# Where the second layer's memory keys and values are computed: in the first layer, or between expert quads

## The chip, the cores and the metric

The kernel runs on one core of a Trainium2 chip. The metric is the device time of one execution in microseconds. Three runs of the kernel before took 991.36, 989.58 and 991.78 us; the median is 991.36 us.

## The reference, cut to what matters

Two transformer layers follow each other on 256 tokens of width 1024. The first has a mixer, a cross attention to a memory of 256 rows and a mixture of 32 experts. The second is a hybrid layer; one of its three branches is a cross attention to another memory, `mem_2`.

```python
def reference(...):
    x = first_block(x, mem, ...)      # mixer, cross attention, experts
    return second_block(x, mem_2, ...)
# in first_block, per layer
    h = h + _mixer(...)
    h = h + _cross_attention(h, mem, ...)          # softmax over 256 rows, 4 heads, then @ w_out
    h = h + _hier_moe(h, ...)                      # router, then hid = silu(xb @ w_gate[e]) * (xb @ w_up[e]); hid @ w_down[e]
# in hybrid_layer
    kv = rmsnorm(mem, g_mem) @ w_mem_kv            # 256 x 1024 by 1024 x 1024
    xk = kv[..., :X_W].reshape(B, M, X_HEADS, X_HEAD_DIM)      # keys: the first 512 columns
    xv = kv[..., X_W:].reshape(B, M, X_HEADS, X_HEAD_DIM)      # values: the last 512
    yc = cross_attention(heads(xq, ...), xk, xv)
```

`xk` and `xv` depend on the inputs alone, so they can be computed at any time before the second layer's cross attention.

## The kernel before

**Dense blocks.** Every dense weight matrix is used in blocks of 1024 x 512 (2 MiB in fp32, two halves of 1 MiB). SP loads the halves, in the order of `FIRST_BLOCKS` and `SECOND_BLOCKS`, into a raw ring (`load_dense`, L694 is its DMA), each when the block two places earlier has been used. ACT rounds a half to a high part (`split_hi`, L1021), VectorE makes the low part (`split_lo`, L1600), and TensorE forms three products: high by high, high by low, low by high (`dense`, L2697 to L2699, or `moving_by_quarters`, L2723 to L2726). A block is 48 matmuls with 512 moving columns, or 96 with 256 where the weights stand (`standing`). The last blocks of the first layer are cq0, cq1 (queries), xk2 (the second layer's memory keys), co0, co1 (output of the cross attention) and xv2 (the second layer's memory values).

**Order on TensorE at the end of the first layer.** The queries are turned and the scores cs formed (L3026). ACT and VectorE make the softmax of four heads in two pairs (maxima L1806, exponentials L1044, weights L2058). Meanwhile TensorE runs xk2, with the transposes of the first two heads' probabilities between its halves (`turn_first_probs`). Four fp32 outputs follow (`co_0` to `co_3`, L3057), then co0 and co1. Then comes xv2, in four quarters. The transposes of the new h, the router's logits (L3079) and the ranks (L3090 to L3094) are put between its steps (`router_before`, `logits_behind`), so that VectorE's router work (L2114 to L2189) goes on beside it. The row norm factors of the memory are spread over partitions by two small matmuls (mrow0, mrow1, L2658).

**Experts.** The 32 experts are worked in eight quads of four. Each expert has room for 32 tokens. A quad's weights are six units of 4 MiB: gate, gate, up, up, down, down (24 MiB a quad). TensorE gathers the tokens (L3127), uses the units (fp32 matmuls, L3155 for gate and up, L3178 for down, 32 records a unit), and scatters the outputs (L3212). There are four unit buffers, so SP (`load_quad`, L735) may issue unit g when unit g - 4 has been used; it learns that from the semaphore `unit_used`. Buffer 1 is used by units 1 of the first quad and 0 of the second; the first two experts' pieces of the second quad's first unit have a place of their own, `ahead`. The first quad's pieces are loaded in parts during the first layer, each as soon as its place is free: `load_piece` (L728), `load_staged` (down weights in places of their own, L760 and L763), `load_part` (L794), the last gate piece (L811) and the last down pieces (L816, L839). L839 is issued when TensorE has used half of the first unit (`first_used`). The remaining piece of the second quad's first unit is issued when the sixth unit is used (L846). SP's queue is worked strictly in order: a wait holds everything behind it.

**After the experts** the second layer's dense blocks follow; xk2 and xv2 are first read near its end.

## Time and profile before

| | value |
|---|---|
| median of three runs | 991.36 us |
| the profiled execution | 989.82 us, span of its instructions 988.0 us |
| TensorE busy | 834.9 us (85%) |
| VectorE, ScalarE, GpSimd busy | 481.3, 335.2, 23.4 us |
| DMA | 294.71 MB, mean 298 GB/s |
| granted TensorE clock, mean | 0.938 |
| chain that ended last | PE 59%, DMA 35%, ACT 2%, DVE 2% |

PE is TensorE, DVE VectorE, ACT ScalarE, POOL GpSimd, SP the queue that issues most DMAs. All times in the rows are microseconds from the start of the span of the profiled execution, which is the one to make sums against. Its time outside the span is 1.8 us. Matmuls are pipelined: the busy time of one (0.39 us for 512 columns) is longer than the distance from one to the next (0.23 us), so stages are measured from start to start. A share of the DMA engines is the part of the time in which the 16 engines had packets, averaged over them.

### The profile page before, as it was taken

To read this page: it belongs to the slowest core of one execution; us is meant where nothing else is said; L and a number is where in the kernel's file an instruction comes from. 1 tells how busy PE (TensorE), PEld (TensorE's weight loads), DVE (VectorE), ACT (ScalarE), POOL (GpSimd) and SP (SyncE) were. 2 spreads that over 40 slices of the span, in tenths; PEclk is the share of its full clock that TensorE was granted. 3 is DMA by queue.
4 is the path that set the end of the run, shared out by engine and by line. 5 is a ranking of instruction groups with operands and counts; after the bars stand their busy time and mean duration, and the time that the engine had idled before them with its cause. 6 is when DMAs were issued, how large, how long until landed. Compare 5 with 4: busy or idle time off the path is not lost.

```text
span 988.0 us, 12917 instructions
## 1 busy us (share of the span) xinstructions
PE 834.9 (85%) x5185; PEld 576.2 (58%) x5185; DVE 481.3 (49%) x946; ACT 335.2 (34%) x560; POOL 23.4 (2%) x35
## 2 busy tenths in 40 slices
PE   8999999999986665757566585747999999999997
PEld 8788888898631211313121131312887899888996
DVE  5788767774611120302003030201867788787695
ACT  5666745854110000101010010001434656455533
POOL 1021010100000000000000000000000000000000
PEclk9999999999997888978888887879999999999999
DMA  8754666597999999999999999999555445453531
GB/s 311 277 171 170 212 223 229 186 410 277 375 429 424 433 429 429 433 429 432 432 428 433 427 431 430 425 436 393 194 170 172 143 155 160 139 170 130 194 130 60
DMA packets 64155, 294.71 MB, mean 298 GB/s; under 512 B 3970, under 2 KB 16996, under 8 KB 55396
## 3 DMA queue, kind: packets, MB, share of 16 engines
q1 hardware_dynamic: 62644, 290.91, 74.9%
q10 hardware_dynamic: 1456, 3.03, 0.8%
q8 instruction: 39, 0.64, 0.3%
q14 instruction: 16, 0.13, 0.0%
HBM read 292.88 MB, written 1.05 MB: 297 GB/s over the span
## 4 chain that ended last, share of the span: by engine, by line
PE 59%; DMA 35%; ACT 2%; DVE 2%; SPq 2%; issue 1%; POOL 0%; POOLq 0%; ACTq 0%; DVEq 0%
DMA uT<-in_down_units 11%; PE bank L2697 10%; PE bank L2699 10%; PE bank L2698 10%; DMA uT<-in_gate_units 10%; DMA uT<-in_up_units 10%; PE bank L3155 5%; PE bank L2762 5%; PE bank L2631 3%; PE bank L3178 3%; PE bank L2764 2%; DMA ring<-in_first_blocks 2%; DMA ring<-in_gate_units 2%; PE bank L3269 1%; PE bank L3476 1%; PE bank L2912 1%
## 5 line engine op out<-in xcount | busy, mean ns | idle before, releaser
L1600 DVE TENSOR_TENSOR ring_rounded<-ring,ring_rounded 128x2048 fp32r<-128x2048 f32 x76 | 174.2, 2292 | 87.1 <-ACT ring_rounded L1021 86.5
L1021 ACT ACTIVATE ring_rounded<-ring 128x2048 fp32r<-128x2048 f32 x75 | 143.6, 1914 | 154.2 <-PE bank L2699 118.9
L3155 PE MATMUL bank<-ring,main 128*32 128x512 f32 x744 | 106.7, 704 | 47.7 <-DMA ring<-in_up_units 43.2
L2699 PE MATMUL bank<-ring_rounded 128*128 128x512 f32 x320 | 124.9, 390 | 0.0
L3155 PEld LDWEIGHTS bank<-ring,main 128*32 128x32 f32 x744 | 27.5, 126 | 115.2 <-issue 92.3
L2697 PE MATMUL bank<-ring_rounded,uT_rounded 128*128 128x512 f32 x208 | 82.8, 398 | 0.7 <-DVE ring_rounded L1600 0.5
L2698 PE MATMUL bank<-ring_rounded,uT_rounded 128*128 128x512 f32 x208 | 81.1, 390 | 0.0
L3178 PE MATMUL bank<-ring,main 128*32 128x512 f32 x352 | 50.5, 726 | 34.4 <-DMA ring<-in_down_units 34.4
L2762 PE MATMUL bank<-stream_pair,ring_rounded 128*128 128x512 f32 x192 | 69.6, 405 | 0.0
L2223 DVE TENSOR_TENSOR normed<-bank,normed 128x512 f32<-128x512 f32 x20 | 13.8, 692 | 110.5 <-PE bank L3212 110.5
L2699 PEld LDWEIGHTS bank<-ring_rounded 128*128 128x128 f32 x320 | 60.1, 188 | 12.9
L2200 DVE SCALAR_TENSOR_TENSOR main<-main,bank 128x512 f32<-128x512 f32 x8 | 5.5, 688 | 125.2 <-PE bank L3155 125.2
L3155 PE MATMUL bank<-main 128*32 128x512 f32 x200 | 40.0, 718 | 22.3 <-DMA uT<-in_up_units 13.5
L2764 PE MATMUL bank<-stream_pair,ring_rounded 128*128 128x256 f32 x192 | 53.8, 280 | 0.0
L1320 ACT ACTIVATE main<-bank 128x512 f32<-128x512 f32 x8 | 4.8, 597 | 143.3 <-PE bank L2631 143.3
L3178 PEld LDWEIGHTS bank<-ring,main 128*32 128x32 f32 x352 | 13.3, 129 | 66.4 <-issue 38.4
L2697 PE MATMUL bank<-ring_rounded 128*128 128x512 f32 x128 | 51.0, 399 | 0.0
L1328 ACT ACTIVATE main<-bank 128x512 f32<-128x512 f32 x16 | 9.6, 598 | 121.6 <-PE bank L3178 121.6
L2698 PE MATMUL bank<-ring_rounded 128*128 128x512 f32 x128 | 49.9, 390 | 0.0
L2697 PEld LDWEIGHTS bank<-ring_rounded,uT_rounded 128*128 128x128 f32 x208 | 39.0, 188 | 11.7 <-DVE ring_rounded L1600 2.1
L2698 PEld LDWEIGHTS bank<-ring_rounded,uT_rounded 128*128 128x128 f32 x208 | 39.1, 188 | 7.4
L2762 PEld LDWEIGHTS bank<-stream_pair,ring_rounded 128*128 128x128 f32 x192 | 36.1, 188 | 10.7 <-issue 2.4
(381 smaller groups left out, 1582.0 us busy)
## 6 DMA issues: line engine op xcount, KB each, us to landing
ring<-in_up_units SPq DMA_DIRECT2D x11, 4096.0 KB, 33.5
ring<-in_w_in SPq DMA_DIRECT2D x42, 1024.0 KB, 5.1
ring<-in_down_units SPq DMA_DIRECT2D x10, 4096.0 KB, 32.2
ring<-in_gate_units SPq DMA_DIRECT2D x9, 4096.0 KB, 33.5
main<-in_gate_units SPq DMA_DIRECT2D x4, 3072.0 KB, 30.3
main<-in_down_units SPq DMA_DIRECT2D x3, 3072.0 KB, 32.6
main<-in_up_units SPq DMA_DIRECT2D x3, 3072.0 KB, 30.4
ring<-in_w_ckv SPq DMA_DIRECT2D x8, 1024.0 KB, 5.1
```

Of the source, the lines that this page charges most:

```text
L1021: a.activation(rounded(hi_half(name, h)), raw_half(name, h), ACT.Copy).then_inc(hi_made, 1)
L1600: v.tensor_tensor(rounded(raw), raw, as_f32(hi_half(name, h)), ALU.subtract).then_inc(split_made, 1)
L2223: ins = v.tensor_tensor(to, b[:, :], to, ALU.add)
L2631: return nc.tensor.transpose(dst, src, ident[0:k, 0:k])
L2697: mm(dst, left[0], right[0], start=first, stop=False, skip_group_check=True)
L2698: mm(dst, left[0], right[1], start=False, stop=False, skip_group_check=True)
L2699: last = mm(dst, left[1], right[0], start=False, stop=last_one, skip_group_check=True)
L2762: mm(b[:, :, :], w_hi[:, k, at], low_and_high(k), start=k == 0, stop=False, skip_group_check=True)
L2764: last = mm(b[:, 1, :], w_lo[:, k, at], x_hi[:, k, :], start=False, stop=k == KC - 1, skip_group_check=True)
L2912: ins = mm(banks[n][:, t * P:t * P + (t + 1) * P], left[on, t * P:(t + 1) * P], right[on, 0:(t + 1) * P], start=t == 0, stop=True, skip_gr ...
L3155: last = mm(bank[2 + part][on, :], xg3[:, h * (KC // 2) + k, on], expert_piece(j, p, u, e, KC)[:, k, :], start=h + k == 0, stop=h * (KC // ...
L3178: ins = mm(bank[4 + half][on, :], hidT3[:, c, on], w[:, half * 512:half * 512 + 512], start=c == 0, stop=c == FC - 1)
```

## The change

The blocks xk2 and xv2 leave the first layer and the plan of dense blocks; `co0` and `co1` each move up in the loads. TensorE computes keys and values as plain fp32 products instead of three products of rounded parts: the keys between quad 0 and quad 1 (`memory_keys`: 32 matmuls of 256 moving columns, after the scatter of quad 0), the values between quad 1 and quad 2 (`memory_values`: 16 of 512 columns). Their weights are loaded by SP in the experts' stream: the keys' 2 MiB into the part of buffer 1 that the second quad leaves free, behind L843; the values' 2 MiB into `ahead`, behind the wait until the second quad's first unit has been used. The last two units of the second quad stand behind that and behind a wait for the finished keys. ACT multiplies the transposed memory by its gain after quad 0, and moves row factors and values; VectorE spreads the factors after quad 0 and moves the keys. So each has its second quad written out ahead of its loop.

The softmax of the cross attention has no dense block beside it any more: the heads are turned and multiplied in pairs. In the router, transposes, logits and ranks follow each other, with 14 and 6 dummy matmuls (`keep_busy`) before the two waits for VectorE. Two copies of h2T go from ACT to VectorE. The rounding of the memory into high and low parts (`raw_hi`, `raw_lo`) goes; the transposed memory lands where the raw copy had its high part.

The places that this frees let SP issue earlier: the first quad's last gate piece (1 MiB) behind cq0, one staged half (0.5 MiB), an up piece (1 MiB) and a whole staged piece (1 MiB) behind co0, and the other gate pieces of unit 1 beside co0 and co1. The banks of PSUM are renumbered by a constant shift (`expert_bank`). The diff, cut to its core:

```diff
-FIRST_PARTS = (4, 8, 4, 8)
+FIRST_PARTS = (4, 5, 4, 8)
...
-                "wo0", "wo1", "cq0", "cq1", "xk2", "co0", "co1", "xv2"]
+                "wo0", "wo1", "cq0", "cq1", "co0", "co1"]
...
+        key_weights = ring[:, 0:SLOT].rearrange("p (k n) -> p k n", k=KC)
+        value_weights = ahead[:, :].rearrange("p (k n) -> p k n", k=KC)
...
+                    sp.dma_start(expert_piece(0, 0, 1, GROUP - 1, KC), of_expert(gate_w, GROUP - 1, 1, KC))\
+                        .then_inc(unit_landed[1], 16)
                 elif name == "co0":
-                    wait_filled(sp, LAST_USE["cq1"])
-                    load_piece(0, 1, gate_w)
+                    load_staged(2, [1])
                     in_order(sp, row_squared, ROW_NORMS, "mem2")
...
+                    load_staged(1)
+            wait_filled(sp, LAST_USE["cq1"])
+            load_piece(0, 1, gate_w)
+            sp.wait_ge(head_summed, len(HEAD_SQUARES))
+            load_staged(0)
+            wait_filled(sp, "cs1_1")
+            load_piece(0, 2, gate_w)
+            load_piece(2, 0, up_w)
+            load_piece(2, 1, up_w)
+            load_staged(3)
+            wait_filled(sp, "co_3")
+            load_piece(0, GROUP - 1, gate_w)
+            load_staged(2, [0])
+            wait_used(sp, "co0", 0)
+            sp.dma_start(weight_unit(1, 0, KC), of_expert(gate_w, 0, 1, KC)).then_inc(unit_landed[1], 16)
+            wait_filled(sp, LAST_USE["co0"])
+            sp.dma_start(weight_unit(1, 1, KC), of_expert(gate_w, 1, 1, KC)).then_inc(unit_landed[1], 16)
             sp.wait_ge(quarter_used, 1)
-            load_part(1, 0, gate_w, 0)
+            load_part(1, 2, gate_w, 0)
+            load_part(3, 0, up_w, 0)
             wait_used(sp, "co1", 0)
-            load_part(1, 0, gate_w, 2)
+            load_part(1, 2, gate_w, 2)
+            load_part(3, 0, up_w, 2)
             load_part(3, 2, up_w, 0)
             load_part(3, 3, up_w, 0)
             sp.wait_ge(quarter_used, 2)
-            load_part(1, 1, gate_w, 0)
+            load_part(3, 1, up_w, 0)
+            load_last_down(0)
             wait_filled(sp, LAST_USE["co1"])
-            load_part(1, 1, gate_w, 2)
+            load_part(3, 1, up_w, 2)
             load_part(3, 2, up_w, 2)
             load_part(3, 3, up_w, 2)
-            def load_last_gate(k):
-
-                sp.dma_start(expert_piece(0, 0, 1, GROUP - 1, KC)[:, k:k + 2, :],
-                             of_expert(gate_w, GROUP - 1, 1, KC)[:, k:k + 2, :]).then_inc(unit_landed[1], 16)
-
-            def load_last_down(k):
-
-                sp.dma_start(expert_piece(0, 0, UNITS - 1, GROUP - 1, FC)[:, k:k + 1, :],
-                             of_expert(down_w, GROUP - 1, 1, FC)[:, k:k + 1, :]).then_inc(early_down_landed, 16)
-
-            sp.wait_ge(quarter_used, 3)
-            load_part(1, 2, gate_w, 0)
-            load_part(3, 0, up_w, 0)
+            load_last_down(1)
...
+            sp.dma_start(key_weights, SOURCE["xk2"]).then_inc(key_weights_landed, 16)
             load_quad(0, 1, 1, (1, 2))
             sp.wait_ge(moe.unit_used, UNITS)
             sp.dma_start(unit_runs(1)[0][:, front:], gate_w[1, 0, :, front:]).then_inc(unit_landed[1], 16)
-            load_quad(0, 1, 1, range(3, UNITS))
+            load_quad(0, 1, 1, (3,))
+            sp.wait_ge(moe.unit_used, UNITS + 1)
+            sp.dma_start(value_weights, SOURCE["xv2"]).then_inc(value_weights_landed, 16)
+            sp.wait_ge(memory_keys_made, 2)
+            load_quad(0, 1, 1, (4, 5))
...
+            for k in range(KC):
+                at = slice(k * T, (k + 1) * T)
+                last = a.activation(mem2T[:, at], mem2T[:, at], ACT.Copy, scale=column("g_mem_2", k))
+            last.then_inc(memory_gained, 1)
+            act.wait_ge(memory_rows_made, 1)
+            a.activation(mem2_rows, expert_bank(6)[:, 0:T], ACT.Copy).then_inc(memory_rows_moved, 1)
+            act_quad(1)
+            wait_rstd(act, "mem2")
+            for t in range(TT):
+                act.wait_ge(memory_values_made, t + 1)
+                a.activation(xv2[:, t * 512:t * 512 + 512], expert_bank(4 + t)[:, :], ACT.Copy, scale=row_of("mem2", t))\
+                    .then_inc(memory_values_moved, 1)
...
+            dve.wait_ge(moe.unit_used, UNITS - 1)
+            spread_rows("mem2", mem2_spread)
+            gathered_high(moe, 1)
+            dve.wait_ge(memory_rows_moved, 1)
+            for half in range(2):
+                dve.wait_ge(memory_keys_made, half + 1)
+                v.tensor_tensor(two_chunks(xkT[:, half * 512:half * 512 + 512]), two_chunks(expert_bank(4 + half)),
+                                by_rows(mem2_rows), ALU.mult).then_inc(memory_keys_moved, 1)
+            dve_quad(moe, 1, 2)
+            with dve.Fori(2, 2 * LAST_PAIR) as i:
...
+            for hp in range(2):
+                for hh in (2 * hp, 2 * hp + 1):
+                    c_turn(hh)
+                for hh in (2 * hp, 2 * hp + 1):
+                    c_out(hh)
...
+            both_drained("co1_0", "co1_1")
+            turn(["h2T2", "h2T3"], h_tok, 2)
+            pe.wait_ge(router_scaled, 1)
+            both_drained("h2T0", "h2T1")
+            wait_free("logits")
+            for k in range(KC):
+                if k in (KC // 2, KC // 2 + 2):
+                    wait_drained(pe, f"h2T{k // 2}")
+                last = logits_of(k)
+            full("logits", last)
+            keep_busy(in_bank("h2T0"), 14)
+            pe.wait_ge(router_step, 1)
+            b = wait_free("rank")
+            mm(b[:, 0:NE], earlier[:, :], assigned[:, 0, :], start=True, stop=True)
+            mm(b[:, NE:2 * NE], ones[:, :], assigned[:, 0, :], start=True, stop=False)
+            mm(b[:, NE:2 * NE], earlier[:, :], assigned[:, 1, :], start=False, stop=True)
+            mm(b[:, 2 * NE:3 * NE], ones[:, :], assigned[:, 0, :], start=True, stop=False)
+            full("rank", mm(b[:, 2 * NE:3 * NE], ones[:, :], assigned[:, 1, :], start=False, stop=True))
+            keep_busy(in_bank("h2T0"), 6)
...
+            def memory_keys():
+
+                pe.wait_ge(moe.added, 8)
+                pe.wait_ge(rows_spread, 2)
+                b = expert_bank(6)
+                for t in range(TT):
+                    last = mm(b[:, t * P:(t + 1) * P], ones[:, :], mem2_spread[:, t * P:(t + 1) * P], start=True, stop=True)
+                last.then_inc(memory_rows_made, 1)
+                pe.wait_ge(moe.y_ready, 2)
+                pe.wait_ge(memory_gained, 1)
+                pe.wait_ge(key_weights_landed, 16)
+                for half in range(2):
+                    b = expert_bank(4 + half)
+                    for c in range(2):
+                        at = (2 * half + c) * P
+                        for k in range(KC):
+                            last = mm(b[:, c * T:(c + 1) * T], key_weights[:, k, at:at + P], mem3[:, k, :],
+                                      start=k == 0, stop=k == KC - 1)
+                    last.then_inc(memory_keys_made, 1)
+                pe.wait_ge(memory_rows_moved, 1)
+                pe.wait_ge(memory_keys_moved, 2)
+
+            def memory_values():
+
+                pe.wait_ge(moe.y_ready, 3)
+                pe.wait_ge(value_weights_landed, 16)
+                for t in range(TT):
+                    for k in range(KC):
+                        last = mm(expert_bank(4 + t)[:, :], mem3[:, k, t * P:(t + 1) * P], value_weights[:, k, :],
+                                  start=k == 0, stop=k == KC - 1)
+                    last.then_inc(memory_values_made, 1)
+                pe.wait_ge(memory_values_moved, 2)
...
+                if in_first_quad(j, 0):
+                    memory_keys()
...
+                    if in_first_quad(j, 0):
+                        memory_values()
```

## Rows read from the trace of the kernel before

**Rows 1.** The page, 40 slices of 24.7 us: DMA share in tenths, GB/s.
```profile
DMA  8754666597999999999999999999555445453531
GB/s 311 277 171 170 212 223 229 186 410 277 375 429 424 433 429 429 433 429 432 432 428 433 427 431 430 425 436 393 194 170 172 143 155 160 139 170 130 194 130 60
```

**Rows 2.** Stretches: length, busy PE, PEld, DVE, ACT, POOL, clock, DMA share, GB/s.
```profile
50.00:75.00 25.00, 25.00 (x155) 20.52 (x153) 20.80 (x34) 16.96 (x23) 5.97 (x2) 1.00 0.51 169
...
265.90:303.70 37.80, 27.48 (x222) 11.43 (x214) 8.78 (x27) 4.49 (x10) 0.00 (x0) 0.93 1.02 426
195.00:265.90 70.90, 70.72 (x445) 61.91 (x447) 42.53 (x106) 31.41 (x58) 2.34 (x2) 1.00 0.92 349
400.00:650.00 250.00, 161.84 (x1037) 58.66 (x1039) 39.83 (x104) 17.19 (x41) 0.00 (x0) 0.85 1.00 430
```

**Rows 3.** Instructions in order of time, PE: start, duration, line, tiles, shape, count.
```profile
200.67 0.28 PE L2697 MATMUL bank<-main_rounded,ring_rounded 128*128 128x256 f32 x1
...
212.89 1.89 PE L3057 MATMUL bank<-main,ring 128*128 128x256 f32 x8
...
220.49 0.58 PE L2697 MATMUL bank<-ring_rounded 128*128 128x512 f32 x1
...
243.39 0.39 PE L2723 MATMUL bank<-ring_rounded,main_rounded 128*128 128x512 f32 x1
...
260.25 3.73 PE L3127 MATMUL bank<-main,h 128*128 128x128 f32 x32
```

**Rows 4.** Instructions in order of time, VectorE and ACT, around the softmax.
```profile
201.68 0.62 DVE L2058 TENSOR_SCALAR main<-main,inv 128x256 f32<-128x256 f32 x2
...
205.49 0.69 DVE L1806 TENSOR_REDUCE maxes<-bank 128x2 f32<-128x512 f32 x1
...
209.00 0.62 DVE L2058 TENSOR_SCALAR main<-main,inv 128x256 f32<-128x256 f32 x2
...
208.65 1.92 ACT L1021 ACTIVATE ring_rounded<-ring 128x2048 fp32r<-128x2048 f32 x1
...
217.53 0.60 ACT L956 ACTIVATE main<-bank 128x512 f32<-128x512 f32 x1
```

**Rows 5.** Instructions in order of time, VectorE and PE, in the router.
```profile
243.59 0.69 DVE L1994 TENSOR_TENSOR h<-bank,h 128x512 f32<-128x512 f32 x1 [0.68 <-PE bank L2726]
...
250.20 0.97 PE L3079 MATMUL bank<-w_router,uT 128*128 128x36 f32 x8
...
252.81 0.42 DVE L2114 SCALAR_TENSOR_TENSOR main<-bank,rstd,b_router 128x36 f32<-128x36 f32 x2 [3.08 <-PE bank L3079]
...
256.24 0.41 PE L3090 MATMUL bank<-assigned,earlier 128*128 128x32 f32 x2
...
257.84 1.75 DVE L2180 TENSOR_SCALAR main<-slot_no,rank,rstd 128x32 f32<-128x32 f32 x8
```

**Rows 6.** Instructions in order of time, SP's queue: issues at F and later.
```profile
265.89 2.99 SPq L839 DMA_DIRECT2D ring<-in_down_units  x6
...
287.84 0.33 SPq L846 DMA_DIRECT2D ring<-in_gate_units  x1
```

**Rows 7.** The chain of waits: start, length, what it waited for.
```profile
287.84 15.86 DMA ring<-in_gate_units
...
303.95 5.83 PE bank L3155 x32
...
340.35 31.95 DMA uT<-in_up_units
```

**Rows 8.** PE in order of time around an idle time, and that stretch's clock.
```profile
346.89 3.64 PE L3155 MATMUL bank<-ring,main 128*32 128x512 f32 x32
...
352.99 5.21 PE L3155 MATMUL bank<-ring,main 128*32 128x512 f32 x32 [2.09 <-DMA ring<-in_gate_units]
...
352.80:356.20 3.40, 3.21 (x16) 0.78 (x20) 0.17 (x1) 0.00 (x0) 0.00 (x0) 0.50 1.00 434
```

**Rows 9.** DMA issues by line: size of each, median time from issue to landing.
```profile
ring<-in_w_in SPq DMA_DIRECT2D x42, 1024.0 KB, 5.1
```

More of the change, by code:

```diff
@@ L140 @@
 LAST_USE = {"gqk": "gqk1", "gv": "gv_1", "dq": "dq_1", "dk": "dk_1", "dv": "dv_1", "gg": "gg_1"}
-for b in ("ck0", "ck1", "cv0", "cv1", "wo0", "wo1", "cq0", "cq1", "co0", "co1", "xk2", "xv2", "iq",
+for b in ("ck0", "ck1", "cv0", "cv1", "wo0", "wo1", "cq0", "cq1", "co0", "co1", "iq",
           "dq2", "dk2", "dv2", "mq", "mk", "mv", "mg", "xq", "dg", "xg", "gl0", "gl1", "gl2", "gl3",
@@ L181 @@
 HI_BANKS += [f"{x}T{c}" for x in ("ck", "h1") for c in range(4)]
-HI_BANKS += [f"{x}T{c}" for half in (0, 2) for x in ("mem2", "cq") for c in (half, half + 1)]
+HI_BANKS += [f"cqT{c}" for c in range(4)]
 HI_BANKS += [f"co_{c}" for c in range(4)] + [f"h3T{c}" for c in range(4)]
@@ L356, in build @@
         c.at = 1792
-        mem2_lo = c.take(2048)
+        last_gate = c.take(2048)
         c_prob += [c.take(512)]
@@ L758, in load_staged @@
                 if i in (1, 3):
-                    whole = mem2T.rearrange("p (k n) -> p k n", k=FC // 2) if i == 1 else normed[:, :, :]
+                    whole = memory_heads.rearrange("p (k n) -> p k n", k=FC // 2) if i == 1 else normed[:, :, :]
                     sp.dma_start(whole, of_expert(down_w, i, 0, FC)).then_inc(staged_landed[i], 16)
@@ L1243, in _ @@
             queries_out(0)
-            split_hi("xk2", [0])
+            split_hi("co0", [0])
             for c2 in (0, 1):
                 query_hi(c2)
-            raw_hi("mem2", mem2T, mem2_lo, "g_mem_2", (2, 3))
             queries_out(1)
@@ L1250, in _ @@
                 query_hi(c2)
-            wait_rstd(act, "mem2")
-            for t in range(TT):
-                copy(f"mrow{t}", mem2_rows[:, t * P:(t + 1) * P], P)
             def pair_exps(kind, t, hp, dsts, scale):
@@ L1278, in _ @@
             c_exps(0)
-            split_hi("xk2", [1])
             c_exps(1)
-            split_hi("co0", [0])
             c_turned(0)
@@ L1327, in expert_out @@
                         act.wait_ge(S.down_done, n + 1)
-                    a.activation(y_slots[:, half * 512:half * 512 + 512], bank[4 + half][:, :], ACT.Copy)\
+                    a.activation(y_slots[:, half * 512:half * 512 + 512], expert_bank(4 + half)[:, :], ACT.Copy)\
                         .then_inc((S.y_first, S.y_ready)[half], 1)
@@ L2068, in _ @@
             pair_weights("c", 1, c_prob)
-            split_lo("xk2", [1])
             pair_bias("c", 2, c_neg(2))
@@ L2073, in _ @@
             pair_weights("c", 3, c_prob)
-            split_lo("co0", [0])
-            wait_drained(dve, "mrow1")
-            for half in range(2):
-                done(f"xk2_{half}", v.tensor_tensor(two_chunks(xkT[:, half * 512:half * 512 + 512]),
-                                                    two_chunks(wait_filled(dve, f"xk2_{half}")), by_rows(mem2_rows),
-                                                    ALU.mult))
             split_lo("co0", [1])
@@ L2090, in _ @@
             v.memset(top_two[:, :, :], 3e38)
-            add_to_h("co", following=("co1", "xv2"))
+            add_to_h("co", following=("co1", None))
+            for c2 in (2, 3):
+                copy(f"h2T{c2}", uT_chunks(c2))
             in_order(dve, row_squared, ROW_NORMS, "h2")
@@ L2096, in _ @@
             _, row0, _ = NORM_AT["h2"]
-            split_lo("xv2", [1])
             rc = Carver(rt, 0, 512)
@@ L3040, in c_turn, with c_out @@
                 four_blocks(f"cpT{hh}", c_prob, hh)
-            def turn_first_probs(h):
-                if h == 1:
-                    c_turn(0)
-                    c_turn(1)
-            pe.wait_ge(inputs_split, 12)
-            standing("xk2", parts(mem2T, mem2_lo), before_half=turn_first_probs)
-            for hh in range(H1):
-                if hh in (1, 2):
-                    c_turn(hh + 1)
+            def c_out(hh):
                 b = wait_free(f"co_{hh}")
@@ L3154, in experts @@
                                 on = slice(e * CAP, (e + 1) * CAP)
-                                last = mm(bank[2 + part][on, :], xg3[:, h * (KC // 2) + k, on],
+                                last = mm(expert_bank(2 + part)[on, :], xg3[:, h * (KC // 2) + k, on],
                                           expert_piece(j, p, u, e, KC)[:, k, :],
@@ L3447, in _ @@
             standing_wide("gl5", first_x)
-            for t in range(TT):
-                wait_drained(pe, f"xv2_{t}")
             x_out(0)
```

143 lines of the change are left out of this document (47 added, 96 removed).

## The prediction

> **What bounds the kernel now.** The slices of the span come first [rows 1]. They show three stages: a first layer in which the DMA engines are 40 to 90% busy, an expert stage from about 270 to 685 us in which they are 90% busy or more and move some 430 GB/s, and a second layer. The table by stretches [rows 2] sharpens this. From 400 to 650 us the DMA share is 1.00 at 430 GB/s with PE busy for 162 of 250 us: transfers set the time. From 195 to 265.9 us PE is busy for 70.72 of 70.9 us while DMA has a share of 0.92 at only 349 GB/s: TensorE sets the time, and the DMA engines follow it. The chain of waits [rows 7] says the same of the experts: 15.86 us, then 31.95 us of it are weights in flight. So a microsecond taken from PE ahead of the experts counts only if the expert transfers also come to their end earlier, and every byte added behind that point is paid.
>
> I call F the moment when PE has used the first half of the first quad's first unit. At F SP issues the last down weights of that quad, at 265.89 [rows 6]. Buffers hold nearly a whole quad, so no more can be loaded ahead of F; from F on DMA is never short of work [rows 2]. The end of the kernel moves by (move of F) + (DMA time added behind F) - (transfers that were still in flight at F).
>
> **PE ahead of F: the cross attention.** xk2 starts at 200.67, the first cross output (L3057) at 212.89, co0 at 220.49 [rows 3]: 19.8 us. In it xk2 is 96 matmuls, 11.35 us after taking off 0.87 for the transposes inside it. It hid the softmax. Without it PE waits. VectorE has the first pair of heads ready at 201.68 + 0.62 = 202.30; the second pair took from 205.49 to 209.62, 4.13 us, and ACT was free of its exponentials at 208.65, 3.16 us after that start [rows 4]. Both now start at 202.30: ACT is free at 205.46, the second pair is ready at 206.43. PE turns the first pair at 202.4 (1.7 us idle, 0.9 busy), then waits until ACT, whose program puts the copies behind all exponentials, has copied it: 205.46 + 0.60 + 0.1 = 206.2 [rows 4] (2.9 us idle). Then come two outputs of 1.73 us, two transposes of 0.44, about 0.5 us for ACT (it has a weight split of 1.92 and two copies ahead of the next one), and two outputs: 8.3 us. co0 starts at 214.5 instead of 220.5: **-6.0 us**, not -11.4. The row-factor matmuls that go (0.5 us) stood in a wait for ACT and give nothing. The lower and upper halves of co0 and co1 are split earlier and stay ahead of PE.
>
> **The router.** co1 ends, and xv2 starts, at 243.39; the gather starts at 260.25 [rows 3]: 16.9 us, of which xv2 is 48 matmuls of 0.23 = 11.1. Without it PE follows VectorE. From the end of co1: the last sum is in h after 0.9 (it starts at 243.59 and takes 0.69), transposes until 1.9, eight logit steps of 0.40 (two took 0.81 at 250.20, to the next matmul) until 5.2, VectorE from 252.81 to 256.24 = 3.4 us until PE may rank, 1.6 us until the slots are selected (256.24 to 257.84), 1.75 us for that [rows 5]: 5.2 + 3.4 + 1.6 + 1.75 = 12.0. So **-4.8 us**, not -11.1. The 14 and 6 dummy matmuls (0.22 each) end before what PE waits for. The gather would start at 249.4 and F comes at 255.1: -10.8 us.
>
> **The clock.** PE is now idle for 4.6 of 5.5 us in the softmax. In the trace an idle time of 2.09 us, after 3.6 us of work, was followed by 3.4 us at the 1.2 GHz level, and 32 matmuls took 5.21 instead of 3.64 us [rows 8]. No such gap exists ahead of 295 us now, so the cost is between 0 and one such stretch, 1.6 us; I take 1.0, since the gap here is the longer one. F moves by **-9.8 us** (-10.8 to -9.2).
>
> **What SP brings forward.** 3.5 MB of expert pieces (the last gate piece, one half of a staged down piece, one up piece, one whole staged piece) move ahead of 195 us, and co1 takes the place of xk2. DMA has room there: 5 tenths in the slice from 173 to 198 us [rows 1] leave some 12 us. Each is queued ahead of a dense block needed two blocks (over 10 us) later. I cost them at nothing; without that cover one piece of 1 MB would cost 2.4 us. The same moves mean that DMA has emptied its queue when F comes: last pieces are issued at about 242.5 and land by 248, and it idles until F. That is where most of the gain is lost.
>
> **DMA behind F.** From F to the landing of the first-unit piece that PE waited for (287.84 + 15.86 = 303.70 [rows 7]) DMA moved 37.8 us x 426 GB/s = 16.1 MB [rows 2]. The units due in that time are 13 MiB = 13.6 MB. The rest, about 2.3 MB or 5.3 us, was in flight at F and is not there now: **-5.3**. The restart of an empty queue is priced by a small load: 1 MiB lands after 5.1 us [rows 9], of which the transfer is about 3.1, so **+2.0**. The two weight blocks are 2 x 2 MiB = 4.19 MB in rows of 2 KB. Dense blocks of that kind have a share of 0.51 at 169 GB/s [rows 2], that is 331 GB/s at full share: 12.7 us; at the experts' 430 GB/s it is 9.7. I take 11.0, since a share read while DMA is half idle includes latency. **+11.0** (9.7 to 12.7).
>
> The Trainium skill, "DMA: Bandwidth & Descriptors", Specifications, holds that transfers of 512 B or more per descriptor run at line rate. By that rule 2 KB rows cost what the experts' rows do, the lower bound of 9.7, and the sum below would be 1.3 us less; the trace's 331 GB/s speaks against it.
>
> **Keys and values between quads.** An fp32 product of 128x256 costs 1.73 / 4 = 0.43 us (the eight records of L3057 [rows 3] are four products, and the transposes of the next head start 1.73 us after them). Keys are 32 of them, 13.9 us; values 16 of double width, 13.9 us. PE has the time if DMA keeps buffers to fill. Keys: the sixth unit is used 21.95 us after F [rows 6]; gather, scatter, the sums, the spread of the row factors and their product add 9: the keys run from F+31 to F+45, their sums move until F+45.7, and quad 1's first unit is used at F+49.3. SP sits on this one for the values' weights, and everything behind them is queued with it (the last two units of quad 1). DMA has by then 17 MiB of units and the keys' weights: 2 + 41.8 + 5.5 = F+49.3. The restart of 2 us is exposed in part or whole: **+1.3** (0 to 2). Values come before quad 2's gather: there unit 0 had no wait and unit 3 landed over 30 us after quad 1 ended (31.95 [rows 7]), while values, moves, gather and unit need about 26. Hidden, with some 5 us to spare. ACT's gain on the 1 MB of memory (eight copies, about 3.5 us) falls under the scatter. In the second layer nothing waits on this sooner than before.
>
> **Sum.** -9.8 - 5.3 + 2.0 + 11.0 + 1.3 = -0.8 us. The profiled execution took 989.82 us (span 988.0); the runs' median is 991.36. Forecast against the median: **990.6 us**. With bounds at their ends the sum runs from -10.8 - 5.3 + 2 + 9.7 + 0 = -4.4 to -9.2 - 5.3 + 2 + 12.7 + 2 = +2.2, thus 987.0 to 993.6.
>
> **Rivals.**
> A. The transfers are cheap and the waits short: weights go at the experts' rate, no slow clock, no gap at the hand-over. -4.4 gives 987.0. If ACT's and VectorE's chain in the softmax is also a microsecond shorter, 986. For it: DMA is saturated there at 430. Against: 331 GB/s of the dense loads.
> B. Slower: the keys hold the hand-over. SP waits for quad 1's first unit, PE does keys first, and my two times are equal, F+49.3. Each microsecond by which PE is later from there is idle DMA and goes to the end. PE stands idle for over 1 us before the keys (sums, spread, product), and quad 1's unit took 5.83 instead of 3.6 us at the low level of the clock. If one or two stretches of 3.4 us at 1.2 GHz fall into the keys, that is +1.7 to +3.4, with the dear bound of the weights 995. If the whole of the keys ran at 1.2 GHz it would be +13.9, 1004; work right before them speaks against it.
> C. The first layer's gain does not appear at all, since the DMA queue and not PE sets F (it had a share of 0.92). Then F stays near 265 and the sum is +9, 1000. PE without idle time up to 287 us speaks against it.
>
> **Chances.** Forecast case (within bounds but near its middle) 0.40; A 0.35; B 0.20; C 0.05. A measurement of this kernel can tell about 0.2%, 2 us, from no change. Faster by more (below 989.4): 0.36; within: 0.37; slower (above 993.4): 0.27, as B, C and a part of the dear bounds. The range is 985.5 to 997.0; the likeliest case's own is 987 to 993.6.
>
> **What would show it.** Of after: co0 starting at 214 to 216; the gather at 249 to 251; DMA share well under 0.5 in the last 7 us before F; keys of 13.9 us ending before 302; a DMA share below 1 around 304 to 307; the last expert weights landing within 2 us of now. Wrong if F is not 9 to 11 us earlier, if 4 MB of weights cost other than 10 to 13 us, or if DMA idles anywhere else behind F.

## The result, and the profile after

The change made the kernel slower: 993.28 us as the median of nine runs (991.67 to 995.33) against 989.84 us of the kernel before (988.91 to 991.78), a ratio of 1.0033 [1.0022, 1.0044], or +3.4 us. Forecast were -0.8 us and 990.6. The forecast stood on the median of three runs of before, 991.36, which nine runs put 1.5 us lower. So the absolute time is only 2.7 us off by luck; the difference is off by 4.2. The profiled execution of after has a span of 991.6 us, 3.6 more than before's 988.0, so the trace shows the whole difference.

The page of after, its 40 slices: TensorE's granted clock, DMA share in tenths, GB/s. They answer to [rows 1].

```profile
PEclk9999999989999798978868878777999999999999
DMA  8754667879699999999999999999655444454531
GB/s 309 277 170 170 213 237 272 296 299 343 244 429 383 441 418 435 434 427 435 430 431 433 426 430 433 424 437 382 205 180 170 134 165 149 149 164 134 189 132 62
```

The slice from 248 to 273 us (the eleventh, 244 GB/s) holds the new idle stretch: DMA has emptied its queue ahead of F. SP's queue shows F, the issue of the last down weights, and the issue of the values' weights, which waits until PE has used quad 1's first unit; it answers to [rows 6].

```profile
258.66 3.19 SPq L842 DMA_DIRECT2D ring<-in_down_units  x6
...
308.04 0.38 SPq L853 DMA_DIRECT2D ahead<-in_w_mem_kv  x1
```

F moved from 265.89 to 258.66, by -7.2 us where -9.8 was forecast. From F to the end of the span it is now 991.6 - 258.7 = 732.9 us; before it was 988.0 - 265.9 = 722.1. So **the change takes 7.2 us off ahead of F and adds 10.8 us behind it.** The stretches show both sides (columns as in [rows 2]: length, busy PE, PEld, DVE, ACT, POOL, clock, DMA share, GB/s).

```profile
200.00:205.00 5.00, 1.26 (x10) 0.86 (x8) 3.77 (x13) 3.26 (x13) 0.00 (x0) 0.85 1.03 403
205.00:210.00 5.00, 4.56 (x11) 3.65 (x12) 3.00 (x5) 3.23 (x5) 0.00 (x0) 0.50 1.00 413
...
245.00:250.00 5.00, 5.00 (x35) 5.00 (x34) 2.91 (x21) 0.36 (x2) 0.00 (x0) 0.71 1.01 406
...
0.00:258.66 258.66, 247.61 (x1381) 208.04 (x1385) 173.35 (x339) 143.84 (x242) 21.57 (x32) 0.98 0.69 252
250.50:259.70 9.20, 8.19 (x72) 5.81 (x75) 7.67 (x37) 1.14 (x4) 0.00 (x0) 1.00 0.04 7
...
300.00:315.00 15.00, 14.17 (x115) 6.20 (x117) 4.95 (x19) 0.98 (x2) 0.00 (x0) 1.00 0.89 353
```

The same stretch of before, without keys between its quads:

```profile
300.00:315.00 15.00, 11.05 (x82) 3.27 (x86) 2.50 (x10) 0.98 (x2) 0.00 (x0) 0.72 1.01 424
```

Three things are to be seen. The clock is 0.50 for the whole of 205 to 210 us, and in the 5 us ahead of it PE was busy for only 1.26 us. DMA idles for the 9.2 us around F. And between 300 and 315 us DMA moves 353 GB/s where before has 424.

**The softmax.** PE in order of time, which answers to [rows 3]; brackets give the idle time ahead and what ended it.

```profile
201.68 1.09 PE L2637 MATMUL bank<-ident,main 128*128 128x128 f32 x8 [1.51 <-DVE main L2062]
205.44 6.12 PE L3054 MATMUL bank<-main,ring 128*128 128x256 f32 x16 [2.67 <-ACT main L964]
211.39 1.04 PE L2637 MATMUL bank<-ident,main 128*128 128x128 f32 x8
212.88 3.69 PE L3054 MATMUL bank<-main,ring 128*128 128x256 f32 x16 [0.46 <-ACT main L964]
216.22 0.58 PE L2703 MATMUL bank<-ring_rounded 128*128 128x512 f32 x1
```

ACT in order of time, the end of its exponentials and the copy that PE waits for.

```profile
204.15 0.56 ACT L1052 ACTIVATE main<-bank,bias,q_scale 128x256 f32<-128x256 f32 x1
204.60 0.21 ACT L1052 ACTIVATION_READ_ACCUMULATOR main<-bank,bias,q_scale 128x1 f32 x1
204.69 1.09 ACT L964 ACTIVATE main<-bank 128x512 f32<-128x512 f32 x2
```

The waits are the forecast ones: 1.5 us for VectorE, 2.7 for ACT, whose copy stands behind all exponentials, 0.5 ahead of the second pair. The first 16 output matmuls take 6.12 us, the second 16 take 3.69: the first ran at the 1.2 GHz level, which lasted from 203.5 to 210.4 us, 6.9 us.

**The router.** PE from the logits to the gather, then VectorE's side of it; they answer to [rows 5].

```profile
240.97 3.67 PE L3082 MATMUL bank<-w_router,uT 128*128 128x36 f32 x32
244.46 5.00 PE L2658 MATMUL bank<-ones,ident 128*128 128x128 f32 x28
249.30 0.31 PE L3099 MATMUL bank<-assigned,earlier 128*128 128x32 f32 x2
...
252.93 3.81 PE L3121 MATMUL bank<-main,h 128*128 128x128 f32 x32 [1.01 <-DVE over_flag L2163]
```

```profile
247.96 0.15 DVE L1623 COPY marks<-ones 128x1 f32<-128x1 f32 x1
...
250.54 0.23 DVE L2149 SCALAR_TENSOR_TENSOR rank<-bank,assigned 128x64 f32<-128x64 f32 x1 [2.21 <-PE bank L3103]
250.80 1.75 DVE L2177 TENSOR_SCALAR main<-slot_no,rank,rstd 128x32 f32<-128x32 f32 x8
252.46 0.18 DVE L2162 TENSOR_REDUCE most<-bank 128x1 f32<-128x32 f32 x1
252.68 0.15 DVE L2163 TENSOR_SCALAR over_flag<-most 128x1 int32<-128x1 f32 x1
```

A second stretch at 1.2 GHz, 244.5 to 247.9 us, fell on the 14 dummy matmuls (28 records). They took 5.0 us and overran what they were to cover: VectorE had set its mark at 247.96, and the ranks began only at 249.30.

**The keys.** The chain of waits, which answers to [rows 7]: start, length, what.

```profile
288.40 0.48 DVE main L1645 x2
288.89 0.14 issue
289.02 0.68 PE bank L3218 x4
289.71 13.82 PE bank L3228 x64
303.52 0.83 issue
304.35 3.64 PE bank L3149 x32
307.99 0.37 PE bank L2637 x2
```

The 32 key products take 13.8 us at full clock. Quad 1's first unit is used at 308.0, F+49.3, as forecast.

**The values.** Their products run from 345.5 to 359.4 us. They cost PE's time but not the kernel's: DMA stays at its full rate, and the next awaited weights are still waited for.

```profile
340.00:420.00 80.00, 66.50 (x396) 26.12 (x388) 15.42 (x46) 8.59 (x19) 0.00 (x0) 0.91 1.01 431
375.81 0.63 PE L3149 MATMUL bank<-main 128*32 128x512 f32 x3 [0.63 <-DMA uT<-in_up_units]
```

That wait is 0.63 us where the prediction saw some 5 us to spare: the values are hidden, but barely.

### The profile page after: what moved, and what is told of

It is laid out like the page before. It is cut to its first block, busy times and chain, and to the rows that moved or that the text cites. A ratio compares the mean times of both kernels' runs of the same rounds, so it can differ in the third digit from the quotient of the medians.

```text
span 991.6 us, 12845 instructions
## 1 busy us (share of the span) xinstructions
PE 851.9 (86%) x5177; PEld 580.8 (59%) x5177; DVE 470.6 (47%) x936; ACT 326.7 (33%) x553; POOL 23.4 (2%) x35
## 4 chain that ended last, share of the span: by engine, by line
PE 61%; DMA 31%; DVE 2%; ACT 2%; issue 2%; SPq 1%; POOL 0%; POOLq 0%; ACTq 0%; DVEq 0%
PE bank L2703 10%; PE bank L2705 10%; PE bank L2704 10%; DMA uT<-in_down_units 9%; DMA uT<-in_gate_units 7%; DMA uT<-in_up_units 7%; DMA ring<-in_down_units 6%; PE bank L3149 5%; PE bank L2768 5%; PE bank L3172 4%; PE bank L2637 3%; PE bank L2770 2%; PE bank L3121 2%; DMA ring<-in_first_blocks 2%; PE bank L3206 1%
## 5 line engine op out<-in xcount | busy, mean ns | idle before, releaser
L1607 DVE TENSOR_TENSOR ring_rounded<-ring,ring_rounded 128x2048 fp32r<-128x2048 f32 x72 | 165.0, 2291 | 85.2 <-ACT ring_rounded L1029 84.6
L1029 ACT ACTIVATE ring_rounded<-ring 128x2048 fp32r<-128x2048 f32 x71 | 135.9, 1914 | 151.0 <-PE bank L2705 119.0
L3149 PE MATMUL bank<-ring,main 128*32 128x512 f32 x744 | 101.2, 680 | 36.2 <-DMA ring<-in_up_units 34.4
L3172 PE MATMUL bank<-ring,main 128*32 128x512 f32 x352 | 60.0, 843 | 33.7 <-DMA ring<-in_down_units 33.7
L2220 DVE TENSOR_TENSOR normed<-bank,normed 128x512 f32<-128x512 f32 x20 | 13.8, 692 | 116.1 <-PE bank L3206 116.1
L2703 PEld LDWEIGHTS bank<-ring_rounded,uT_rounded 128*128 128x128 f32 x208 | 39.0, 188 | 11.3 <-DVE ring_rounded L1607 1.5
```

Of the source, the lines that this page charges most:

```text
L1029: a.activation(rounded(hi_half(name, h)), raw_half(name, h), ACT.Copy).then_inc(hi_made, 1)
L1607: v.tensor_tensor(rounded(raw), raw, as_f32(hi_half(name, h)), ALU.subtract).then_inc(split_made, 1)
L2220: ins = v.tensor_tensor(to, b[:, :], to, ALU.add)
L2703: mm(dst, left[0], right[0], start=first, stop=False, skip_group_check=True)
L3149: last = mm(expert_bank(2 + part)[on, :], xg3[:, h * (KC // 2) + k, on], expert_piece(j, p, u, e, KC)[:, k, :], start=h + k == 0, stop=h * ...
L3172: ins = mm(expert_bank(4 + half)[on, :], hidT3[:, c, on], w[:, half * 512:half * 512 + 512], start=c == 0, stop=c == FC - 1)
```

## The experiments

In all of them one number does most of the work: the span less F. Where only what lies ahead of F is edited, it should not change. "Scores to co0" is from the last score matmul's start to co0's first matmul; "logits to gather" is from the first logit matmul to the first gather matmul; all from the profiled executions, us. After was timed in its own session and not again beside the variants, so they are compared through the ratios to before. The two intervals together leave such a difference uncertain by 1.4 to 1.7 us; span less F, from the traces, is the sharper measure (732.6 to 732.9 in the five kernels in which nothing behind F differs).

| kernel | scores to co0 | stretch at 1.2 GHz there | logits to gather | F | span - F |
|---|---|---|---|---|---|
| before | 19.93 | none | - | 265.89 | 722.1 |
| after | 16.33 | 6.9 | 11.96 | 258.66 | 732.9 |
| e1_fill_softmax | 13.88 | none | 10.92 | 254.86 | 732.7 |
| e2_copies_first | 13.26 | 3.4 | 10.92 | 253.86 | 732.6 |
| e3_router_8_dummies | 15.56 | 3.4 | 10.92 | 256.50 | 732.6 |
| e4_split_unit | 16.49 | 6.9 | 11.95 | 259.63 | 730.5 |
| e5_rows_16k | 16.76 | 6.9 | 11.95 | 259.05 | 732.0 |
| e6_no_weights | 15.59 | 3.4 | 11.96 | 257.41 | 727.7 |
| e8_later_f | 16.40 | 6.9 | - | 262.32 | 732.7 |
| e9_no_weights_few_products | 16.90 | 6.9 | 11.95 | 259.57 | 720.2 |
| c1_copies_dummies_split_rows | 12.59 | none | 10.92 | 254.45 | 729.5 |
| c2_copies_split | 12.61 | none | 10.91 | 253.55 | 730.6 |

My theory M: F sets the end, the waits in the softmax are ACT's order of work, the slow clock costs more than I took, and behind F each block pays its products or its transfer, whichever is longer, and a hole at the hand-over. Rivals: the clock is not the cause, or the transfers cost more than their bytes (in part D in the expectations).

**e1_fill_softmax: give PE something to do in the two waits.**

```diff
+            filler = wait_free("co_0")
+            keep_busy(filler, 6)
             for hp in range(2):
@@
+                if hp == 0:
+                    keep_busy(filler, 11)
```

> The changed kernel (993.3 us, before 989.8) with 6 dummy matmuls ahead of the first turn of the cross attention's probabilities and 11 between that turn and the first output, in TensorE's two waits. Theory M (TensorE sets F, F sets the end, and the softmax gap costs a stretch at 1.2 GHz): the clock stays at 2.4 GHz, the first two outputs take 3.5 us as before instead of 6.1, F comes 2.5 us earlier, time 990.8. Rival D (the DMA queue, not F, sets the end): the outputs are faster but the time stays at 993.3. Rival K (dummies overrun their waits): no stretch at 1.2 GHz, F less than 1 us earlier, 992.5 to 993.5.

Measured: 990.46 us, ratio 1.0015 [1.0006, 1.0023] against before, which had 989.09 beside it. At after's ratio of 1.0033 after would be 992.35 there, so e1 takes off 1.9 us, give or take 1.4. PE in order of time:

```profile
199.72 1.50 PE L2658 MATMUL bank<-ones,ident 128*128 128x128 f32 x12
201.34 1.09 PE L2637 MATMUL bank<-ident,main 128*128 128x128 f32 x8
202.27 2.62 PE L2658 MATMUL bank<-ones,ident 128*128 128x128 f32 x22
205.11 3.69 PE L3054 MATMUL bank<-main,ring 128*128 128x256 f32 x16 [0.21 <-ACT main L964]
```

The outputs start as long after the scores as in after (5.52 us against 5.55), so the waits are the same; but they take 3.69 us instead of 6.12, and no stretch at 1.2 GHz is left in the softmax or the router. That prices the clock in the softmax at 16.33 - 13.88 = 2.45 us, in the router at 11.96 - 10.92 = 1.04 us. The slow clock is shown as a cause. The timed gain is smaller than these 3.5 us of two profiled executions, though not beyond its uncertainty. Since the stretches differ from execution to execution (table), after need not have both at full length in each of them; that is a reading, not shown.

**e2_copies_first: let ACT copy the first pair before it takes the second pair's exponentials.**

```diff
             c_exps(0)
-            c_exps(1)
             c_turned(0)
             c_turned(1)
+            c_exps(1)
```

> The changed kernel with one move in ACT's program: the copies of the first two heads' turned probabilities stand ahead of the second pair's exponentials. Theory M: TensorE's second wait (2.7 us) shrinks to about 0.7, the idle time no longer brings the clock down, co0 starts some 4 us earlier (212 instead of 216.2), F 4 us earlier, time 989.3. If only the wait goes and the clock still falls, F is 2 us earlier and the time 991.3. Rival D: 993.3.

Measured: 988.87 us, ratio 0.9998 [0.9989, 1.0007]: 3.5 us under after, and as fast as before. PE in order of time:

```profile
200.94 1.09 PE L2637 MATMUL bank<-ident,main 128*128 128x128 f32 x8 [1.51 <-DVE main L2062]
202.38 5.38 PE L3054 MATMUL bank<-main,ring 128*128 128x256 f32 x16 [0.34 <-ACT main L964]
```

The wait of 2.67 us is down to 0.34. It was not data that PE lacked but the copies' place in ACT's program. The slow stretch is down from 6.9 to 3.4 us in the softmax and gone from the router, though I had expected either no drop and 989.3, or a drop and 991.3. The path from the scores to co0 is 3.1 us shorter and the router's 1.0; how much of this is the wait and how much the clock, the run does not separate.

**e3_router_8_dummies: fewer dummies in the router.**

```diff
-            keep_busy(in_bank("h2T0"), 14)
+            keep_busy(in_bank("h2T0"), 8)
```

> The changed kernel with 8 instead of 14 dummy matmuls between logits and ranks. In its trace the 14 took 4.8 us, since the clock was at 1.2 GHz from 244.5 to 247.9, and TensorE came to the ranks 1.2 us after VectorE was ready. Theory M: ranks start at VectorE's mark, F and the end 1.2 us earlier, 992.1. Rival N (the dummies are needed): the ranks are no later, but the gather and the first unit run in a stretch at 1.2 GHz and F is 0.5 to 2 us later, 994 to 995. Rival D: 993.3.

Measured: 992.46 us, ratio 1.0034 [1.0021, 1.0047]: no gain is seen, but the 1.2 us expected lie within the uncertainty. The profiled execution had no slow stretch in the router, but e1 and both c kernels have none with 14 dummies either. So it is not shown that the number of dummies matters. What the slow clock does with 14 of them is shown by after.

**e4_split_unit: half of quad 1's fifth unit goes out ahead of the wait for the hand-over.**

```diff
+            sp.wait_ge(memory_keys_made, 2)
+            sp.dma_start(unit_runs(1)[0][:, 0:2 * HALF], down_w[1, 0, :, 0:2 * HALF]).then_inc(key_weights_landed, 16)
             sp.wait_ge(moe.unit_used, UNITS + 1)
             sp.dma_start(value_weights, SOURCE["xv2"]).then_inc(value_weights_landed, 16)
-            sp.wait_ge(memory_keys_made, 2)
-            load_quad(0, 1, 1, (4, 5))
+            sp.dma_start(unit_runs(1)[0][:, 2 * HALF:], down_w[1, 0, :, 2 * HALF:]).then_inc(unit_landed[1], 16)
+            load_quad(0, 1, 1, (5,))
```

PE waits for `key_weights_landed` at 32 where it uses that half.

> The changed kernel with half of the second quad's fifth unit (the part whose place the key weights had) issued as soon as the keys are made, ahead of SP's wait for that quad's first unit. Theory M: the hole in the DMA work at 307.6 to 309.1 closes, the end comes 1.5 us earlier, 991.8. Rival H (the hole is made up later, since TensorE's use of the units and not DMA paces that stretch): no hole, but 993.3.

Measured: 990.82 us, ratio 1.0014 [1.0005, 1.0022], 1.5 to 1.9 us under after by the medians and the ratio. Its stretch at the hand-over:

```profile
300.00:315.00 15.00, 14.17 (x111) 6.78 (x113) 4.95 (x19) 0.98 (x2) 0.00 (x0) 1.00 0.97 408
```

Against after's 353 GB/s this is 55 GB/s x 15 us = 0.83 MB more, 1.9 us at 430 GB/s. F was even later than after's, 259.63, and span less F fell from 732.9 to 730.5. By this the hole at the hand-over costs 2.4 us; the timing says 1.9, give or take 1.4.

**e8_later_f: PE later by 22 dummies ahead of the gather.**

```diff
-            keep_busy(in_bank("h2T0"), 6)
+            keep_busy(in_bank("h2T0"), 28)
```

> The changed kernel with 22 more dummy matmuls before the gather of the first quad, 4.9 us at 2.4 GHz, of which 1 us falls into a wait: F comes 4 us later. Theory M (F sets the end, DMA idles 9 us ahead of it): 996.4. Rival D (the end is set by DMA's total, a later F is made up from the units that have landed): 992.4 to 994.

Measured: 996.77 us, ratio 1.0072 [1.0059, 1.0085]; before had 989.36 beside it, so after would be 992.6: +4.2. F is 3.7 us later in the trace, and span less F is 732.7. PE sets F and F sets the end; rival C of the prediction falls.

**e5_rows_16k: the keys' and values' weights in rows of 16 KB.**

```diff
-        SOURCE["xk2"] = block_cols(A["w_mem_kv_2"], 0)
-        SOURCE["xv2"] = block_cols(A["w_mem_kv_2"], 512)
+        SOURCE["xk2"] = A["mem_kv_2"][:, 0:SLOT].rearrange("p (k n) -> p k n", k=KC)
+        SOURCE["xv2"] = A["mem_kv_2"][:, SLOT:2 * SLOT].rearrange("p (k n) -> p k n", k=KC)
```

> The changed kernel (992.4 us beside a before of 989.1) with the key and value weights laid out so that a partition's 16 KB lie in one run, as the experts' weights do; bytes and order unchanged. The trace's 2 KB packets took 88 ns, 372 GB/s, so each block should cost 4.9 instead of 5.6 us. Theory M (TensorE's path from F to the second quad's first unit takes 49.3 us and hides the keys' weights; only what lies behind it counts): the values' block alone gives back 0.7 us, 991.7. Rival D (every microsecond of DMA behind F counts): 1.5 us, 990.9. Rival Z (2 KB rows go at the experts' rate): 992.4.

Measured: 992.64 us, ratio 1.0031 [1.0019, 1.0043]: no change that the timing can tell. Span less F is 0.9 us shorter. That is nearer to the 0.7 which M expects for the values alone than to D's 1.5, but the kernels that differ only ahead of F scatter by 0.3, so it favours M and does not settle it; e6 does.

**e6_no_weights: no loads of the keys' and values' weights; the products read what lies there.**

```diff
-            sp.dma_start(key_weights, SOURCE["xk2"]).then_inc(key_weights_landed, 16)
...
-            sp.dma_start(value_weights, SOURCE["xv2"]).then_inc(value_weights_landed, 16)
```

> The changed kernel without the loads of the key and value weights and the waits for them (keys and values are products of what lies in those places, so the output is not the reference's). 4.19 MB fewer. Theory M: without the keys' weights DMA only waits longer for SP's go after quad 1's first unit (a hole of 7 us instead of 1.5), so that only the values' 5.6 us come back, 986.8. Rival D (the stream's bytes set the end): 11.3 us, 981.1.

Measured: 987.03 us, ratio 0.9979 [0.9971, 0.9988], 5.6 us under after, and span less F falls by 5.2. That is about one block's transfer, not two; M had forecast 986.8 and D 981.1. The stretch ahead of the hand-over in e6 says why:

```profile
300.00:302.00 2.00, 2.00 (x11) 1.67 (x9) 0.00 (x0) 0.00 (x0) 0.00 (x0) 1.00 0.38 164
302.00:304.00 2.00, 1.17 (x12) 0.38 (x14) 1.69 (x7) 0.00 (x0) 0.00 (x0) 1.00 0.00 0
304.00:306.00 2.00, 2.00 (x24) 0.75 (x20) 0.66 (x4) 0.00 (x0) 0.00 (x0) 1.00 0.04 8
```

Without the keys' weights DMA is done by about 301 us and idles until PE has used the unit at 306.87 (SP's next issue), F+49.5. The keys' transfer lies beside work of PE that must be waited for anyway.

**e9_no_weights_few_products: as e6, and 4 instead of 32 key products.**

```diff
-                        for k in range(KC):
+                        for k in range(1):
```

> As the one without weights, and with 4 of the 32 key products (one per sum; the output is not the reference's). TensorE reaches quad 1's first unit 12 us earlier. Theory M: now neither the keys' transfer nor their products hold anything, the end comes 11.3 + 1.5 us earlier than in the changed kernel, 979.6. Rival P (the products cost nothing even without the weights): as the one without weights alone, 986.8 or 981.1, whichever that shows.

Measured: 981.66 us, ratio 0.9924 [0.9912, 0.9936]: 5.4 us under e6, and its span is 5.3 us shorter though its F, with the longer slow stretch, came 2.2 us later. The unit is used at F+41.8, 7.7 us earlier, and span less F falls by 7.5 to 720.2, 1.9 us under before's 722.1. With the keys' weights away, their products cost 7.5 us behind F. M had expected 12 us earlier for the unit and 979.6 for the time. The trace shows what took the rest: PE now waits for weights, and the unit itself falls into a slow stretch (5.34 us instead of 3.64).

```profile
295.92 0.62 PE L3147 MATMUL bank<-ahead,main 128*32 128x512 f32 x2 [3.56 <-DMA ring<-in_gate_units]
295.92 5.34 PE bank L3147 x32
```

The products alone were not taken out with the weights kept. As an estimate, the keys' transfer of 5.6 us (its 2 KB packets at 372 GB/s) put on top of F+41.8 would give F+47.4 against F+49.4, so it would have gained about 2 us: the two ways are nearly equally long, and taking one away alone gives little.

**c2_copies_split and c1_copies_dummies_split_rows: the parts together.** c2 is e2 and e4. c1 is c2 with e5's rows, and the dummies of e1 with 4 instead of 11 in the second wait.

> Two of these edits alone: the copies and the split unit. Theory M (one shortens TensorE's path to F, the other closes the hole behind it, so they add): 992.4 - 3.5 - 1.9 = 987.0. Rival D (they overlap): 988.9, as the copies alone.

> Four edits together: copies ahead of the second pair's exponentials, 6 and 4 dummy matmuls in what is left of the two waits, the second quad's fifth unit split, key and value weights in 16 KB runs. Against a before of 989.1 the changed kernel is at 992.4. Theory M: 3.5 us (copies) + 1.9 (split) as measured alone, + 1.7 for the stretch at 1.2 GHz that the dummies prevent, + 0.7 to 1.5 for the runs now that the hand-over does not wait: 984.5, faster than both kernels. Rival D (the parts overlap): 987 to 988.

Measured: c2 986.77 us, ratio 0.9974 [0.9965, 0.9984]; c1 985.68 us (985.16 to 985.85), ratio 0.9961 [0.9948, 0.9975]. c2 is where M had it (987.0), so its two parts add up. c1 beats both kernels, 3.9 us under before, but is 1.2 us short of M's 984.5, which had counted 1.7 us for a slow stretch that c2's profile does not have. Its softmax, by stretches:

```profile
200.00:205.00 5.00, 4.87 (x39) 4.58 (x39) 3.08 (x10) 3.40 (x13) 0.00 (x0) 1.00 1.02 367
205.00:210.00 5.00, 3.82 (x23) 3.23 (x22) 3.60 (x7) 5.00 (x12) 0.00 (x0) 1.00 1.01 400
```

Full clock throughout. c1 and c2 have the same softmax (12.6 us) in their profiles, where c2 had no slow stretch either; the 1.1 us between their spans less F (730.6 and 729.5) are the rows'. Every run of c1 is faster than every run of c2. c1's runs lie within 0.7 us, c2's within 2.2. That the dummies keep the clock up in every execution would explain it, but was not tried apart.

## Why the prediction was wrong

The mechanism held step by step: PE sets F, DMA follows, buffers are full ahead of F so that the gain there turns into idle DMA, and behind F bytes and the hand-over are paid. Its sizes were off, and most of the errors leaned to one side. By the prediction's own test it was wrong at F, which came 7.2 us earlier and not 9 to 11; the keys ended at 303.5 instead of before 302 for the same reason.

| term | forecast | measured | from |
|---|---|---|---|
| start of the softmax | 0 | -0.7 | scores end at 199.89 + 0.11 instead of 200.67 |
| softmax at full clock | -6.0 | -6.05 | e1: 13.88 instead of 19.93 |
| router at full clock | -4.8 | -4.0 | e1: co0 to F 41.39 instead of 45.40 |
| clock | +1.0 | +3.5 | after against e1: 2.45 and 1.04 |
| F | -9.8 | -7.2 | SP's queue |
| in flight at F | -5.3 | -3.7 | bytes landed by F |
| restart | +2.0 | +1.3 | bytes moved in the 10 us after F |
| 4.19 MB of weights | +11.0 | +10.8 to +11.3 | c2 against c1; their packets |
| hole at the hand-over | +1.3 | +1.9 to +2.4 | e4 |
| sum | -0.8 | +3.1 to +4.1 | span: +3.6 |

**The step that failed most is the clock.** Its cost was put at +1.0 us with 1.6 as its bound, and it measured +3.5. I read one row, a stretch of 3.4 us after an idle time of 2.09 us [rows 8], and made its cost, 1.6 us, the upper bound of the whole. The stage had three waits in 13 us instead of one, and the stretch at 1.2 GHz lasted twice as long: 6.9 us, at a cost of 2.45. I also priced a drop in one place only: the router, where PE is never idle for over 1 us, got its own, of 3.4 us at a cost of 1.04. The rows gave no bound for either; one stretch per new wait would have been the honest one. The Trainium skill, "TensorE: Matmul & The Clock Gate", HAM oscillation — how this bites in real kernels, describes a kernel whose clock fell again at each wait and which paid for it in the work behind the wait. The trace agrees on where the cost falls: 6.12 us behind the wait for outputs that take 3.69. It does not show a fall at each wait: one stretch began in the second wait, and the third brought none.

**In flight at F.** From 0 to F the tables of stretches give 255 GB/s x 265.89 us = 67.8 MB before, and 252 x 258.66 = 65.2 MB after. Before's had 4.19 MB of the memory's weights among them, so 65.2 - 63.6 = 1.6 MB more of the rest had landed, 3.7 us at 430 GB/s. The two rates are rounded, so this is good to about half a microsecond. I had taken all that DMA moved until the awaited piece landed, less the units due; part of the excess belonged to pieces queued behind it. Counting what had landed by F would have avoided that. The sum had a slip too: 16.1 - 13.6 MB are 2.5 and not 2.3, which would have made the term -5.8 and the miss larger.

**The router** was 0.8 us short: the slots' selection is followed on VectorE by two more operations that the gather waits for (L2162 and L2163, ended at 252.83), which I had left out, 0.3 us; I haven't split up the rest.

**The restart** was sized too high. DMA moves its first bytes 1.0 us after F and is slow at first. In the 10 us after F it moves 355 GB/s where before has 410: 0.55 MB less, or 1.3 us.

```profile
265.89:275.89 10.00, 10.00 (x94) 2.96 (x90) 3.08 (x13) 0.98 (x2) 0.00 (x0) 1.00 1.02 410
258.66:268.66 10.00, 10.00 (x94) 2.96 (x90) 3.08 (x13) 0.98 (x2) 0.00 (x0) 1.00 0.92 355
```

**The hole** was taken as part of one restart, 0 to 2 us. DMA runs at its full rate until 307, a microsecond before SP gives it the next work, and is not back at it until 310.

```profile
306.00:307.00 1.00, 1.00 (x16) 0.39 (x12) 0.00 (x0) 0.00 (x0) 0.00 (x0) 1.00 0.99 426
307.00:310.00 3.00, 3.00 (x30) 0.84 (x26) 1.59 (x8) 0.38 (x1) 0.00 (x0) 1.00 0.32 74
```

3 us at 74 instead of 430 GB/s are 2.5 us lost, which agrees with the 2.4 us of e4. So PE's and DMA's ways to F+49.3 were not equal: DMA was about 1 us ahead, and the wait for SP and the restart both showed.

**The weights** came out as forecast. The keys' 2 KB packets took 88 ns, which is 372 GB/s over 16 engines and 11.3 us for both blocks, if packets do not overlap; the values' took 92 ns. The 1.1 us between c2 and c1 give 9.7 + 1.1 = 10.8 us. By the rule of the Trainium skill for 512 B and more, which the prediction names, it would be 9.7 us; the packets and the step from c2 to c1 both decide against it. But this is not what the two transfers cost at the end. e6 shows that the keys' part hides under PE's way to F+49.5, and e9 that the products are what stands there. The term came out right since both ways were nearly equally long, which the prediction saw but used only for the hole. That is luck in part: the sum counts the keys' bytes, and what stands there are their products.

**The rivals.** A (cheap transfers, short waits, no slow clock) is refuted by the slow stretches and the dearer 2 KB rows. B had the right sign and place: the hand-over did cost more than forecast, but not by a slow clock in the keys, which ran at 1.00; the loss lies in the DMA hole. C is refuted by e8. The largest part of the miss was in none of them: no rival let the slow clock eat the gain ahead of F. Its two stretches are worth 2.5 us more than taken, which turns the sum from -0.8 to +1.7; the in-flight term adds 1.6.

What stays open: why the router has its slow stretch in some executions and not in others, and how often each kernel's executions have it; the traces are one for each kernel. The in-flight and restart terms are read from bytes moved; no run changed them alone.

## What to carry to other kernels

Before work is taken out of an engine, ask what it covered: here 11 us of products hid a softmax, and taking them out gave 3.6 us, since waits and a slow clock came in their place. Then look at the order inside the engine that is now waited for: two copies moved ahead of the exponentials gave back as much as the whole change had lost. A block that moves into a stage bound by transfers takes its bytes along, and a wait put on the issuing queue there costs an empty queue besides; give that queue something to send first (e4).

## What the runs showed of the hardware

- In the softmax the 1.2 GHz level of TensorE came in stretches of 3.4 or of 6.9 us, for the same instructions and waits: e3 and e6 had the short one in the softmax, after, e4, e5, e8 and e9 the long one. Measured from e1's 13.88 us, the short one costs 1.7 us there, the long one 2.4 to 3.0. e2 and c2 run the same softmax too; e2's profile has a stretch of 3.4 us, c2's none.
- A second stretch, of 3.4 us, came in the router in six of these seven, on logit matmuls of 36 columns or the dummies behind them, where PE had not been idle for more than 0.83 us; in none of the four kernels whose softmax waits were filled or shortened.
- Dummy matmuls that are counted for full clock run twice as long at 1.2 GHz and then delay what they were to cover: 28 records took 5.00 us here, and cost 1.04.
- Packets of 2 KB took 88 ns, 372 GB/s over 16 engines, in the very stage in which the experts' larger rows move at 430; laying 4.19 MB out in rows of 16 KB gave 1.1 us (c2 against c1).
- A wait of the issuing queue, with DMA saturated on both sides of it, cost 2.4 us: DMA moved 74 GB/s for 3 us.
